# Layer two of a hybrid block: GpSimd gates each expert block's output, TensorE adds H to the second tile's sums, the closing operations read PSUM and send half tiles

## The reference

```
u2 = h * (1 + sc2) + sh2
f  = sum over the token's two experts e of gate_e * ((silu(u2 @ Wg_e) * (u2 @ Wu_e)) @ Wd_e)
h  = layer_norm(alpha * h + g2 * f, ln2_g, ln2_b)      # the output, 256 x 1024
```

## Time and profile before

| | before |
|---|---|
| median of 3 runs | 1777.48 us (1769.59 to 1777.82) |
| profiled execution, its own time | 1775.91 us |
| its span in the trace | 1774.1 us |
| busy over the span: TensorE, VectorE, ScalarE, GpSimd | 91%, 44%, 21%, 12% |
| mean granted clock of TensorE | 0.97 of full speed |
| layer two's block loop in the trace | from 1510 to 1757 us |
| from the last block's copy to the end of the span | 1755.5 to 1774.1 us |

### The profile page before, as it was taken

The page is one execution under the profiler, slowest core; times in us unless marked ns, Lnnn a source line. Parts: engine busy times, 40 slices in busy tenths (PEclk is TensorE's granted clock), DMA queues, the critical chain, the costliest instruction groups (busy, mean ns, idle before and its releaser), DMA issues.

```text
span 1774.1 us, 31200 instructions
## 1 busy us (share of the span) xinstructions
PE 1614.8 (91%) x12950; PEld 976.2 (55%) x12950; DVE 778.1 (44%) x1536; ACT 365.3 (21%) x889; POOL 206.4 (12%) x220
## 2 busy tenths in 40 slices
PE   4999998899999999889999895999789997999984
PEld 2454475444444458655555444768568886555542
DVE  3059725365101012544236546494461115564555
ACT  1101025542000010412222212013631012111111
POOL 0200000000000000023333221000000000343321
PEclk8999999999999999999999998999999998999997
DMA  9523645730321332689569988432003564999994
GB/s 311 162 95 119 213 153 181 261 107 5 107 71 38 104 132 78 222 343 407 194 218 398 406 356 263 139 101 83 24 1 112 187 217 166 348 408 400 407 385 190
DMA packets 180446, 359.77 MB, mean 203 GB/s; under 512 B 13777, under 2 KB 100153, under 8 KB 179795
## 3 DMA queue, kind: packets, MB, share of 16 engines
q1 hardware_dynamic: 170592, 330.43, 51.7%
q0 software_dynamic: 8800, 22.93, 3.6%
q10 hardware_dynamic: 915, 4.42, 0.6%
HBM read 352.79 MB, written 10.35 MB: 205 GB/s over the span
## 4 chain that ended last, share of the span: by engine, by line
PE 63%; issue 13%; DVE 7%; DMA 6%; POOL 5%; ACT 4%; SPq 0%; POOLq 0%; DVEq 0%; ACTq 0%
PE psum L912 61%; DMA yab<-in_moe_w_gu 4%; POOL ys L866 2%; POOL qkT L849 2%; DMA ring<-in_w_mod 2%; PE psum L974 1%; ACT arena L1665 1%; PE psum L1370 1%; ACT arena L1662 1%; DVE hstat L2001 1%; PE psum L1397 0%; DVE arena L2051 0%; PE psum L1132 0%; DVE ring L2296 0%; ACT arena L1616 0%
## 5 line engine op out<-in xcount | busy, mean ns | idle before, releaser
L912 PE MATMUL psum<-uT,ring 128*128 128x512 f32 (+1 forms) x1440 | 489.5, 499 | 0.0
L912 PEld LDWEIGHTS psum<-uT,ring 128*128 128x128 f32 x1440 | 273.4, 191 | 210.7 <-issue 193.9
L912 PE MATMUL psum<-ring,mo_tok 128*32 128x256 f32 x4992 | 308.9, 384 | 19.6 <-DVE ring L2296 18.3
L912 PEld LDWEIGHTS psum<-ring,mo_tok 128*32 128x32 f32 x4992 | 151.4, 110 | 133.8 <-DVE ring L2296 34.7
L912 PE MATMUL psum<-ring,v_tok 128*32 128x256 f32 x2496 | 155.4, 390 | 1.5 <-DVE ring L2296 1.2
L2296 DVE COPY ring<-yab 128x1024 f32<-128x1024 f32 x120 | 86.5, 759 | 124.1 <-PE psum L912 104.8
L1923 DVE SCALAR_TENSOR_TENSOR convT<-upad,cwT,convT 128x512 f32<-128x512 f32 (+1 forms) x240 | 132.4, 614 | 2.1
L2130 DVE TENSOR_TENSOR arena<-psum,mqk 128x512 f32<-128x512 f32 (+1 forms) x16 | 8.9, 558 | 253.6 <-PE psum L912 253.6
L2296 DVE COPY ring<-arena 128x1024 f32<-128x1024 f32 x120 | 81.3, 719 | 86.6 <-PE psum L912 63.7
L912 PE MATMUL psum<-ring,uT 128*128 128x256 f32 (+1 forms) x576 | 113.7, 357 | 0.0
L912 PEld LDWEIGHTS psum<-ring,v_tok 128*32 128x32 f32 x2496 | 76.8, 112 | 64.8 <-issue 19.3
(11 more groups left out here) (319 smaller groups left out, 1500.1 us busy)
## 6 DMA issues: line engine op xcount, KB each, us to landing
yab<-in_moe_w_gu SPq DMA_DIRECT2D x120, 512.0 KB, 10.0
uT<-in_moe_w_gu SPq DMA_DIRECT2D x120, 512.0 KB, 11.1
arena<-in_moe_w_dn SPq DMA_DIRECT2D x120, 512.0 KB, 9.7
ring<-in_w_in SPq DMA_DIRECT2D x104, 512.0 KB, 4.6
ring<-in_w_mod SPq DMA_DIRECT2D x96, 512.0 KB, 6.3
ring<-in_w_out SPq DMA_DIRECT2D x16, 512.0 KB, 4.5
ring<-in_moe_w_gu SPq DMA_DIRECT2D x16, 512.0 KB, 7.8
ring<-in_w_a_out SPq DMA_DIRECT2D x8, 512.0 KB, 3.5
```

The source lines that it names most:

```text
L912: return nc.tensor.matmul(dst, lhsT, rhs, start=start, stop=stop)
```

## The change

It touches layer two only. GpSimd multiplies each block's output by g2 in place (`gate_output`, after `hidden` and the gather), and `add_to_tokens(b)` waits for that. For this g2 is laid out like the block's output, 128 x 256, by 8 matmuls of 32 columns and one copy. Before the last block's `add_to_tokens`, TensorE adds H of the second tile to that tile's sums by 4 matmuls with the identity. At the end VectorE adds the first tile's sums to H; for the second tile the statistics and the first normalising operation read PSUM. Both tiles are finished and sent in halves of 512 channels.

```diff
-        order += [("g2", l, c) for c in range(nt) if l]
+        order += [("g2", l, 0)] if l else []
...
-        g2_last = upad[:, :, :, :].rearrange("p a b c -> p (a b c)")[:, D:2 * D]
+        g2_groups = norm_g[:, DEPTH - 1, 0:2 * P]
...
 (SP)
             for t in range(2):
-                sp.wait_ge(h_ready, sum(NORM_TILES) - 1 + t)
-                sp.dma_start(out[0, t * P:(t + 1) * P, :], H[:, t, :]).then_inc(out_sent, 16)
-            sp.wait_ge(out_sent, 32)
+                for half in range(2):
+                    cols = slice(half * 512, half * 512 + 512)
+                    sp.wait_ge(h_ready, sum(NORM_TILES) - 1 + 2 * t + half)
+                    sp.dma_start(out[0, t * P:(t + 1) * P, cols], H[:, t, cols]).then_inc(out_sent, 16)
+            sp.wait_ge(out_sent, 64)
...
 (GpSimd)
+                def gate_output(b):
+
+                    pool.wait_ge(down_drained, base + b + 1)
+                    nc.gpsimd.tensor_tensor(y_blk[:, b % 2, :], y_blk[:, b % 2, :], g2_groups, ALU.mult)\
+                        .then_inc(block_gated, 1)
+
                 if l == 0:
                     hidden(0)
+                else:
+                    wait_drained(pool, "g2", l, 0)
                 for b in range(nb):
                     if l:
                         block_to_token(b)
                         hidden(b)
                         if b % QUAD == 0 and b // QUAD + 2 < nquad:
                             gather_quad(b // QUAD + 2)
+                        gate_output(b)
                         continue
...
 (TensorE)
+                def gate_row_groups():
...
+                    for j in range(2):
+                        for q in range(QUAD):
+                            last = mm(bank("g2", l, 0)[q * CAP:(q + 1) * CAP, j * P:(j + 1) * P],
+                                      modT[:, l, G2 + 2 * q + j, 0:1].broadcast_to([P, CAP]), ident[:, :])
+                    done(last, "g2", l, 0)
...
-                    gate_rows(1, G2)
+                    gate_row_groups()
...
                 def add_to_tokens(b):
 
-                    pe.wait_ge(down_drained, base + b + 1)
+                    pe.wait_ge(block_gated, b + 1)
                     pe.wait_ge(to_token_ready, b + 1)
...
                 else:
+                    pe.wait_ge(rows_used, 2 * l + 2)
+                    for q in range(QUAD):
+                        mm(token_bank(1, q), ident[:, :], H[:, 1, q * 2 * P:(q + 1) * 2 * P], False, False)
                     add_to_tokens(nb - 1)
...
 (ScalarE)
-                    gate_rows(1)
+                    wait_ready(act, "g2", l, 0)
+                    f(g2_groups, bank("g2", l, 0)[:, 0:2 * P], ACT.Copy).then_inc(drained_of("g2", l, 0), 1)
...
 (VectorE)
-            for t in range(2):
-                add_experts(t)
-                statistics(t).then_inc(ln_var, 1)
+            dve.wait_ge(block_added, QUAD * n_blocks[DEPTH - 1])
+            for q in range(QUAD):
+                last = v.tensor_tensor(H[:, 0, quarter(q)], H[:, 0, quarter(q)], token_bank(0, q), ALU.add)
+            link(last)
+            statistics(0).then_inc(ln_var, 1)
+            for q in range(QUAD):
+                last = v.bn_stats(st4[:, 6 * q:6 * q + 6], token_bank(1, q))
+            link(last)
+            v.bn_aggr(mv[:, 1, :], st4).then_inc(ln_var, 1)
             dve.wait_ge(ln_loaded, 32 * (2 * DEPTH + 1))
             for t in range(2):
                 dve.wait_ge(ln_var, norm_halves(2 * DEPTH) + t + 1)
-                link(v.scalar_tensor_tensor(H[:, t, :], H[:, t, :], mv[:, t, 0:1], ln_g, ALU.subtract, ALU.mult))
+                if t == 0:
+                    link(v.scalar_tensor_tensor(H[:, t, :], H[:, t, :], mv[:, t, 0:1], ln_g, ALU.subtract, ALU.mult))
+                else:
+                    for q in range(QUAD):
+                        last = v.scalar_tensor_tensor(H[:, t, quarter(q)], token_bank(t, q), mv[:, t, 0:1],
+                                                      ln_g[:, quarter(q)], ALU.subtract, ALU.mult)
+                    link(last)
                 dve.wait_ge(ln_std, norm_halves(2 * DEPTH) + t + 1)
                 link(v.reciprocal(rstd[:, t:t + 1], sd[:, t:t + 1]))
-                v.scalar_tensor_tensor(H[:, t, :], H[:, t, :], rstd[:, t:t + 1], ln_b, ALU.mult, ALU.add).then_inc(h_ready, 1)
+                for half in range(2):
+                    cols = slice(half * 512, half * 512 + 512)
+                    v.scalar_tensor_tensor(H[:, t, cols], H[:, t, cols], rstd[:, t:t + 1], ln_b[:, cols], ALU.mult, ALU.add)\
+                        .then_inc(h_ready, 1)
```

More of the change, by code:

```diff
@@ L451, in build @@
         staging = [buf[:, 2 * x:2 * x + 2, :].rearrange("p a b -> p (a b)") for buf in (yab, uT, arena) for x in range(4)]
+        st4 = gate_cols[:, 0, 0:24]
         ln_rows = mo_tok[:, :, :, :].rearrange("p a b c -> p (a b c)")
@@ L528, in build @@
         first_told = sem("first_quad_told")
+        block_gated = sem("block_output_gated")
         to_token_ready, block_added = sem("block_to_token_ready"), sem("block_added_to_tokens")
@@ L1249, in gate_rows @@
                         done(last, *key)
+                def gate_row_groups():
+                    for g in gate_groups(l):
+                        wait_drained(pe, "modt", g)
+                    wait_bank(pe, "g2", l, 0)
+                    for j in range(2):
[3 more added lines that the diff above has]
+                    done(last, "g2", l, 0)
                 gate_rows(0, G1)
@@ L1691, in gate_rows @@
                         wait_ready(act, *key)
-                        dst = g2_last if which and l else g_rows[c // 2]
-                        f(dst[:, (c % 2) * 512:(c % 2 + 1) * 512], bank(*key)[:, :], ACT.Copy)\
+                        f(g_rows[c // 2][:, (c % 2) * 512:(c % 2 + 1) * 512], bank(*key)[:, :], ACT.Copy)\
                             .then_inc(drained_of(*key), 1)
@@ L2302, in add_experts @@
                     y = y_tok[t][:, 0:D]
[L2303 to L2312, removed]
                     dve.wait_ge(gathered[t], 16 * (l + 1))
@@ L2324, in _, with quarter @@
                         norm_half(2 * l + 2, h)
-            for t in range(2):
-                add_experts(t)
-                statistics(t).then_inc(ln_var, 1)
+            def quarter(q):
+                return slice(q * 2 * P, (q + 1) * 2 * P)
+            dve.wait_ge(block_added, QUAD * n_blocks[DEPTH - 1])
[7 more added lines that the diff above has]
+            v.bn_aggr(mv[:, 1, :], st4).then_inc(ln_var, 1)
             dve.wait_ge(ln_loaded, 32 * (2 * DEPTH + 1))
```

## The result

The changed kernel takes 1834.13 us (median of 4 runs, 1831.59 to 1838.51) against 1776.18 us of the kernel before in the same comparison (4 runs): a ratio of 1.0336, 95% interval 1.0311 to 1.0361. The direction was right; the size, +58 us, lies outside the range, above its upper end of 1818 us. The profiled execution of the changed kernel took 1838.51 us, 62.6 more than that of before.

What follows compares the result with a forecast made beforehand. GpSimd's hidden product was taken to bound the block loop, the weight stream the last experts. Terms +25.8 - 2.5 + 0.8 - 2.5 = +21.6 us on 1775.91 gave 1797.5 us, range 1782 to 1818.

Steps and rivals of the forecast that it cites:

- What bounds the kernel: Layer two's block loop: TensorE waits only for GpSimd's hidden product until 1707 us; afterwards the weight stream sets the time.
- the stream covers it: Rival: the weight stream really holds the block loop, so the gate eats idle time; 1774 us, chance 0.13.
- The path per block: Output copy to hidden transposes, now through gate, matrix and hidden: 3.88 us against 2.85, so 1.03 us more per block.
- The matrix: 1.22 alone, 1.47 beside copies; 1.35: GpSimd's block_to_token behind the gate, in each block: priced at 1.35 us, with 1.47 as its high end.
- the loop's term: Delay of the hidden transposes in blocks 1 to 25 at 1.03 us each: +25.8 us.
- GpSimd and VectorE hold each other up: Rival: three GpSimd operations stretched by VectorE's ring copies lose 2.2 us per block; 1826 us or more, chance 0.14.
- The estimate of 0.74 us for the gate: Gate in each block by the reference's figure: 0.74 us, loss 0.62 us per block, time about 1787 us.
- The last blocks: After the last weight part: the last block's hidden product starts 2.6 us after the output copy, not 1.82; +0.8 us.
- The end: Closing work: VectorE starts 1.66 us later, its work is 3.5 us shorter, the last DMA saves 0.65; together -2.5 us.
- The gate rows ahead of the loop: Laying out g2 before the block loop: hidden by TensorE's 5.11 us wait for VectorE's routing; 0 us.
- the stream's: Weight stream from 1707.11 us to its last copied part: a slower loop has worked off the backlog, -2.5 us.

Runs made afterwards that it cites:

- e3: The changed kernel with VectorE copying only 16 of 1024 columns of each staged weight part in layer two; 1781.62 us in one run.
- e4: The changed kernel with 4 more matmuls per layer-two block, results unused, in TensorE's idle time; 1815.96 us, ratio 1.0222 to the kernel before.
- e6: The changed kernel with the next block's matrix built ahead of the gate, and the gate applied twice in a row; 1794.60 us, ratio 1.0108 to before.
- e1: The changed kernel with GpSimd building the next block's matrix ahead of the gate; 1773.08 us, ratio 0.9979 to the kernel before.
- e2: The changed kernel without the gate, adding waits for the output copy as before, result lacks g2; 1778.06 us in one run.

## Why the prediction was right in direction and wrong in size

- **What bounds the kernel: right.** GpSimd's `hidden` product was the last thing TensorE waited for, the weight stream did not cover the added delay, and it idled meanwhile (242 to 326 GB/s). The rival 'the stream covers it' is out: over 25 blocks all of the delay arrives at the end, less 2.2 us (2.5 predicted).
- **The path per block: mechanism right, terms mis-sized.** Predicted 1.03 us per block, measured 1.52. The gate was taken at 1.15 and measures 0.78; `hidden` at 0.75, measured 0.64; the matrix at 1.35, measured **2.42**. The first of the two failing steps is the sentence 'The matrix: 1.22 alone, 1.47 beside copies; 1.35', and with it the high end 1.47. In the earlier trace rows the matrix begins half a microsecond ahead of the copies and has them beside it only in part; behind the gate it has them beside it for 1.9 us or more in 20 of the 26 blocks. The trace of before held two such blocks, which I had read and set aside as odd:

```profile
1580.08 3.18 POOL L841 TENSOR_SCALAR qkT<-mqk 128x256 f32<-128x256 f32 x1 [1.25 <-PE psum L912]
...
1594.78 2.77 POOL L841 TENSOR_SCALAR qkT<-mqk 128x256 f32<-128x256 f32 x1 [2.67 <-PE psum L912]
```

  In both VectorE's copies (from 1578.72 and 1594.00 us) were under way when the matrix began. At 2.42 instead of 1.35 the loop's term would have been some 52 us, where GpSimd's part grew by 38.0: gate and `hidden` were priced 0.49 us too high per block, and that hid 12 us of the error by luck. The rival 'GpSimd and VectorE hold each other up' (1826 us, chance 0.14) was the nearest; but it spread the stretch over all three operations, where it fell on one. The rule of the Trainium skill that I weighed there (Advanced Engine Details and Errata, VectorE Performance Modes, Mode Summary: the port is shared, and two-port Vector instructions and GpSimd interfere or block each other) is borne out as far as the interference goes: 1.22 us without the copies, 2.42 on average with them. A full block does not show: the matrix at 1664.11 took 2.28 us, all of it beside copies of 0.76 us each, so both went on together. The estimate of 0.74 us for the gate, worked out from the figure that the Trainium skill's GPSIMD Engine Reference (Performance versus the Vector engine) gives for an addition of two inputs, is borne out too: 0.73 us in all blocks of e3 but one. It was nearer than my 1.15.
- **TensorE's clock: left out.** This is the second failing step. The prediction has no term for it and gives no reason; it took TensorE's part as unchanged. It measures +0.76 us per block, 19 us, a third of the whole, and e4 shows that the idle time brought it. Idle time was predicted ('grown by about 1 us per block'), and what it would do to the clock wasn't asked. The earlier trace rows held the sign: from 1707 to 1736 us, where TensorE was busy 20.35 of 29 us, the granted clock was 0.89.
- **The last blocks.** Predicted +0.8, measured +3.4 us: the matrix stood there too, 2.14 us beside the last copies.
- **The end.** Predicted -2.5, measured -1.9 us. The H matmuls are on the path as forecast (VectorE starts 1.9 us later, 1.66 forecast); the operations reading PSUM are a little longer than taken (1.65 for the four gains, 1.45 taken).
- **The gate rows ahead of the loop: right**, nothing: from L2151's instruction to the first row numbers there are 31.9 us before and 31.6 after.

In sum the prediction lacks, against the profiled execution: 12.3 us in GpSimd's part, 19.0 in TensorE's, 2.6 in the last blocks, 0.9 in the stream's and the end's terms, and 6.1 that lie ahead of the change and are taken as chance. Neither failing step alone would have left the range: 1797.5 us and the 12.3 missing in GpSimd's part make 1810, with the 19.0 of the clock instead 1817; with both it is 1829, beyond 1818.

## What to carry to other kernels

On an in-order queue, place an added instruction by what stands behind it: work whose inputs are ready early (here the next block's matrix) goes ahead of the one that must wait, and the same instructions cost 3.4% in the one order and nothing in the other. Price an instruction by the rows in which it lies beside what it will lie beside after the move, odd rows first. Where a change adds idle time to TensorE in a loop, add a term for its clock, read from TensorE's part of a block at either level.

## What the runs showed that I had not expected

- TensorE stood idle 1.7 us per block ahead of the hidden transposes (44.7 us in 26 waits), and in stretches of the loop the granted clock fell to 0.83 to 0.91. In e3, with 0.35 us of such idle time in most blocks, it stayed at 1.00, and in e4, where matmuls filled the idle time, as well. In e6, with 0.7 to 1.0 us in most blocks, it was 0.95 from 1611 to 1635 us and 1.00 in most of the loop.
- Beside back-to-back copies of 128x1024 the 128x256 `TENSOR_SCALAR` of GpSimd went from 1.22 to between 2.3 and 2.7 us, the two-input product of the same size only from 0.73 to between 0.8 and 1.06 (e1, e6 and the changed kernel).
- The time ahead of the block loop differs from execution to execution, also between kernels whose instructions up to there are nearly the same: `hidden` of block 0 starts at 1507.8 us (e1), 1515.2 (before), 1516.9 (e2) and 1521.1 (changed). What happens in the loop is better read from its own intervals than from the totals of single runs.

Open stays why the clock of the changed kernel fell in some stretches of the loop and not in others. It was 1.00 from 1627 to 1677 us and from 1733 to 1793 us. Each of these stretches holds two blocks in a row in which the matrix took only 1.66 and 1.56 us, with few copies beside it, so that TensorE's idle time was 0.9 and 1.1 us; but each also holds at least one block with the usual 1.8 us.
